# One order of the weight conversions for every block, single-block experts included

## The chip, the cores and the metric

The kernel runs on one core of a Trainium2 chip. The time is that of one execution on the device in microseconds (us). Three runs of the kernel before gave 2883.24, 2887.31 and 2889.01 us, median 2887.31 us. The profile is of one execution of its own, which took 2882.61 us.

## The reference, cut to what matters

The program is one layer of a diffusion backbone. A token mixer (gated DeltaNet and a gMLP) comes first and isn't touched by the change. The second sub-layer is a mixture of experts, and the change is in its loop. 1024 tokens of width 1024 each choose 4 of 32 experts, the assignments are sorted by expert and cut into blocks of one expert each, and every block is computed as

```python
gu = xblk @ w_gu[e] + b_gu[e]              # 1024 -> 2048
gate = jnp.minimum(gu[:, ::2], SWIGLU_LIMIT)
up = jnp.clip(gu[:, 1::2], -SWIGLU_LIMIT, SWIGLU_LIMIT)
act = (up + 1.0) * gate * jax.nn.sigmoid(SWIGLU_ALPHA * gate)
return act @ w_down[e] + b_down[e]         # 1024 -> 1024
```

The results are scaled by the gates and added up per token. All of it is float32.

## The kernel before, in words

**Blocks.** A block holds 64 rows of one expert. With these inputs there are 82 blocks for 32 experts. The experts are ordered so that busy and little used ones alternate: 7, 1, 7, 1, 6, 1, 5, 1, 4, 1, 3, 1, 3, 1, 3, 1, 3, 1 blocks, and then 3 and 2 in turn, and 2. So nine experts have a single block (blocks 7, 15, 22, 28, 33, 37, 41, 45 and 49, counted from 0), and each stands between two with more blocks. A block that is the first of its expert is called new here.

**Precision.** TensorE multiplies in float16 with each operand split into a high and a low half, and three products for each (high by high, high by low, low by high). So each weight chunk of 1 MB that arrives from memory in float32 is converted twice: ScalarE (ACT) writes its high half (line 1147 for gate-up, line 1153 for down), and after that VectorE (DVE) writes the low half as the difference (lines 1686 and 1691). An expert has 8 gate-up chunks, `k` from 0 to 7, and 4 down chunks. The halves of only one expert are held: the high half of chunk `k` may be overwritten when TensorE has done chunk `k` of the last block that used the old one.

**Loads.** SyncE (SP) issues the loads, strictly in order: gate-up chunks at line 587 into five staging buffers, down chunks at line 591 into four. A chunk's load goes out when the low half of the chunk that was last in its staging buffer is written. After an expert's chunks 5, 6 and 7 (which wait for its own low halves 0, 1 and 2) come chunks 3, 4, 0, 1, 2 of the next expert, in this order, each behind the low half 3, 4, 5, 6 or 7 of the expert before it.

**Turns.** Each engine runs the same loop over blocks, turn `t` from 1, with its own order of work.
- TensorE (PE): the 8 chunks of gate-up of block `t` (lines 2192 to 2194), the transposes of the gathered rows of block `t + 1` (line 2180), the transposes of the result of an earlier block (line 2219), then the 4 down chunks of block `t - 1` (lines 2209 to 2211). Gate-up of a block waits for the low half of each chunk, for its rows (`copy_xT`) and for VectorE's reading of the block before it.
- VectorE, with block `t + 1` as the one read: low halves of block `t + 2` if that one is new; the reading of gate-up (`read_gate_up`, line 1724); the clamps and the product of SwiGLU (lines 1730 to 1734); further low halves of `t + 2`; low halves of down of block `t + 1` if that one is new.
- ScalarE: the row index of a later gather; high halves of `t + 2`; `copy_xT` (line 1171), which can run once TensorE has transposed; more high halves; SiLU (line 1179), which waits for VectorE's first clamp; the remaining high halves; the high half of the activation (line 1184); the copies of results (lines 1189, 1196); high halves of down of `t + 1`, for a block with no new one behind it ahead of line 1184, otherwise at the end of the turn.
- GpSimd (POOL): the gather of rows (line 803), the low half of the activation (line 816), the scatter of results (line 810).

**The two orders.** `new1` says that block `t + 1` is new and `new2` that block `t + 2` is. The chunks of `t + 2` are converted in turn `t` only if `new2` is 1. With `new1` 0, ScalarE converts chunks 0 to 3 ahead of `copy_xT`, chunk 4 ahead of the SiLU, 5 to 7 behind it; VectorE converts 0 to 3 ahead of the reading and 4 to 7 behind SwiGLU. With both 1 (block `t + 1` is a single) ScalarE converts chunk 0 ahead of `copy_xT`, chunk 1 ahead of the SiLU and 2 to 7 behind it, and VectorE chunk 0 ahead of the reading and 1 to 7 behind SwiGLU. Each call of `next_gate_up` is a branch on its condition.

Of the kernel before, what the change touches and what calls it, by code (L numbers as in the profile page):

```python
# [41 lines left out]
GK, DK = 8, 4  # L42
# [71 lines left out]
def hybrid_block(nc, x, c, ctx_in, c_ctx, w_ada, b_ada, norm_g, w_in, conv_w, a_log, dt_bias,  # L114
# [3 lines left out]
    with es:  # L118
# [720 lines left out]
        def _(act):  # L839
# [293 lines left out]
            def flag(t):  # L1133
                return act.value_load(meta[0:1, bass.ds(t + NEW_AT, 1)], min_val=0, max_val=1)

            def rank_before(t):
                return act.value_load(rank_of[0:1, bass.ds(t - 1, 1)], min_val=0, max_val=NE - 1) + 1

            def flags_and_ranks(t):
                code = act.value_load(code_of[0:1, bass.ds(t, 1)], min_val=0, max_val=256 * NE - 1)  # L1140
                new1, new2, r1 = (code >> 1) & 1, (code >> 2) & 1, ((code >> 3) & (NE - 1)) + 1
                return new1, new2, r1, r1 + new1

            def high_gate_up(t, r, k):
                act.wait_ge(s_gst[k % GS], (r * 2 + (k // GS)) * 16 + 16 if k % GS + GS < GK else r * 16 + 16)
                reached(act, s_gu, t, GK, k + 1 - GK)
                act.activation(ghi[k], gstage[k % GS].rearrange("p (f b) -> p b f", b=2), ACT.Copy,  # L1147
                               scale=WSCALE).then_inc(s_ghi, 1)
# [7 lines left out]
            def next_gate_up(t, wanted, r, part):  # L1156
                with act.If(wanted):
                    for k in part:
                        high_gate_up(t, r, k)
                act.sem_inc(s_idle, 1)  # L1160

            def next_down(t, wanted, r):
                with act.If(wanted):
                    for j in range(DK):
                        high_down(t, r, j)
                act.sem_inc(s_idle, 1)

            def copy_xT(t):
                act.wait_ge(s_tx, t + 1)
                reached(act, s_gu, t, GK, 0)  # L1170
                act.activation(xT, ps[:, BX, :].bitcast(F16).rearrange("p (j k t) -> p j k t", j=2, k=KD),  # L1171
                               ACT.Copy).then_inc(s_xc, 1)

            def name_rows(t):
                act.activation(idx[:, 0:1], slots[:, bass.ds(t, 1)], ACT.Copy).then_inc(s_ix, 1)

            def sigmoid(t):
                act.wait_ge(s_gc, t + 1)
                act.activation(sig_n, gate_n, ACT.Silu, scale=ALPHA / WSCALE).then_inc(s_sig, 1)

            def high_act(t):
                act.wait_ge(s_a, t + 1)
                reached(act, s_dn, t, DK, DK)
                act.activation(ah, act_n, ACT.Copy).then_inc(s_ah, 1)  # L1184

            def copy_yT(t):
                act.wait_ge(s_dn, t * DK + 2 * DK)
                reached(act, s_ty, t, 1, EMPTY)
                act.activation(yT, ps[:, BT, :].rearrange("p (c t) -> p c t", c=8), ACT.Copy,  # L1189
                               scale=1.0 / (ALPHA * WSCALE * WSCALE)).then_inc(s_yT, 1)  # L1190

            def scale_y(t):
                act.wait_ge(s_ty, t + (EMPTY + 1))
                reached(act, s_ys, t, 16, 0)
                act.activation(idx[:, 1:2], slots[:, bass.ds(t, 1)], ACT.Copy)
                act.activation(ysb[0:B, :], ps[0:B, BY:BY + 2, :].rearrange("p b c -> p (b c)"), ACT.Copy,  # L1196
                               scale=gtab[:, bass.ds(t, 1)]).then_inc(s_yc, 1)
# [53 lines left out]
            new2, r2 = flag(2), rank_before(2)  # L1251
# [8 lines left out]
            with act.Fori(1, MAXB) as t:  # L1260
                with act.If(t <= nprev):
                    new1, new2, r1, r2 = flags_and_ranks(t)
                    act.wait_ge(s_xg, t * 16 + 48)
                    act.sem_inc(s_idle, 1)
                    name_rows(t + 3)
                    next_gate_up(t + 2, new2 > 0, r2, range(1))
                    next_gate_up(t + 2, new2 > new1, r2, range(1, 4))
                    copy_xT(t + 2)
                    next_gate_up(t + 2, new2 + new1 > 1, r2, range(1, 2))
                    next_gate_up(t + 2, new2 > new1, r2, range(4, 5))  # L1270
                    sigmoid(t + 1)
                    next_gate_up(t + 2, new2 + new1 > 1, r2, range(2, 5))
                    next_gate_up(t + 2, new2 > 0, r2, range(5, GK))
                    next_down(t + 1, new1 > new2, r1)
                    high_act(t + 1)
                    copy_yT(t)
                    scale_y(t - 1)
                    next_down(t + 1, new1 + new2 > 1, r1)
# [16 lines left out]
        def _(dve):  # L1295
# [110 lines left out]
            for m in range(NG - G_QKV):  # L1406
# [16 lines left out]
                if 0 <= j < NQK:  # L1423
                    ct, (t0, n) = j // 3, SPANS[j % 3]
                    dve.wait_ge(s_rt, ct + 1)
                    r, t = norm[ct % 2][:, NORM0[j % 3]:NORM0[j % 3] + n], qkvT[:, ct, t0:t0 + n]
# [257 lines left out]
            def low_gate_up(r, k):  # L1684
                dve.wait_ge(s_ghi, r * GK + (k + 1))
                dve.scalar_tensor_tensor(glo[k], gstage[k % GS].rearrange("p (f b) -> p b f", b=2), WSCALE, ghi[k],  # L1686
                                         ALU.mult, ALU.subtract).then_inc(s_glo, 1)
# [6 lines left out]
            def flag(t):  # L1694
                return dve.value_load(meta[0:1, bass.ds(t + NEW_AT, 1)], min_val=0, max_val=1)

            def next_gate_up(t, wanted, r, part, old=0):
                with dve.If(wanted):
                    for k in part:
                        low_gate_up(r, k)  # L1700
                if old:
                    with dve.Else():
                        dve.wait_ge(s_glo, t * GK + part[0])
                        dve.sem_inc(s_glo, old)
# [52 lines left out]
            new2, r2 = flag(2), rank_before(2)  # L1757
# [5 lines left out]
            with dve.Fori(1, MAXB) as t:  # L1763
                with dve.If(t <= nprev):
                    code = dve.value_load(code_of[0:1, bass.ds(t, 1)], min_val=0, max_val=256 * NE - 1)
                    new1, new2, r1 = (code >> 1) & 1, (code >> 2) & 1, ((code >> 3) & (NE - 1)) + 1
                    r2, e = r1 + new1, (code >> 8) & (NE - 1)
                    next_gate_up(t + 2, new2 > 0, r2, range(1), GK)
                    next_gate_up(t + 2, new2 > new1, r2, range(1, 4))
                    read_gate_up(t + 1, e)  # L1770
                    swiglu(t + 1)
                    next_gate_up(t + 2, new2 + new1 > 1, r2, range(1, 4))
                    next_gate_up(t + 2, new2 > 0, r2, range(4, GK))
                    next_down(t + 1, new1, r1)
                    dve.sem_inc(s_idle, 1)
# [487 lines left out]
```

## Time and profile before

| | |
|---|---|
| runs, median (lowest to highest) | 2887.31 us (2883.24 to 2889.01) |
| the profiled execution | 2882.61 us, span 2880.8 us |
| TensorE matmul, busy | 2584.2 us, 90% of the span |
| TensorE weight load, busy | 2238.8 us, 78% |
| VectorE, busy | 1755.5 us, 61% |
| ScalarE, busy | 1550.8 us, 54% |
| GpSimd, busy | 761.7 us, 26% |
| DMA | 536.74 MB, 186 GB/s over the span |

A busy share is the time in which an engine had an instruction at work, over the whole span. Matmuls are pipelined, so their mean duration is longer than the distance from one to the next. The chain of waits counts, for the instruction that ended last, what released each step; since it is the one that ended last, it says little about a loop in the middle of the program, and the views of single stretches say more.

### The profile page before, as it was taken

How to read it: one execution, taken by the hardware profiler on the slowest of the kernel's cores; microseconds unless marked ns; L12 is line 12 of the kernel's file. 1: busy time of each engine (PE TensorE's matmuls, PEld its weight loads, DVE VectorE, ACT ScalarE, POOL GpSimd, SP SyncE). 2: the span in 40 equal slices, each digit the busy share in tenths (PEclk: the TensorE clock that was granted, in tenths of full speed). 3: DMA queues.
4: the chain of work that ended last, by engine and by line, in shares of the span. 5: the costliest groups of instructions: out<-in, count | busy, mean ns of one | idle time of the engine just before them, and what ended most of it. 6: DMA issues, size and time to landing. Idle time of an engine off the chain costs nothing. (4 is left out here: it accounts for less than half of the span.)

```text
span 2880.8 us, 132861 instructions
## 1 busy us (share of the span) xinstructions
PE 2584.2 (90%) x55873; PEld 2238.8 (78%) x55873; DVE 1755.5 (61%) x1936; ACT 1550.8 (54%) x1833; POOL 761.7 (26%) x586
## 2 busy tenths in 40 slices
PE   8999997898898886699999999998889999999993
PEld 2444556788888754598998998988888999999993
DVE  2344894544545477517264638577787767878883
ACT  3522543433333543517264647577777767768773
POOL 1201003543544212112222222232222322233221
PEclk9999998999999997799999999999999999999997
DMA  9500001000000222818365659698899887979975
GB/s 366 192 30 32 1 1 37 19 26 15 18 25 15 84 96 104 341 24 285 119 209 192 227 173 342 219 329 319 316 351 308 307 291 272 326 276 350 348 276 194
DMA packets 124477, 536.74 MB, mean 186 GB/s; under 512 B 12541, under 2 KB 13553, under 8 KB 91617
## 3 DMA queue, kind: packets, MB, share of 16 engines
q1 hardware_dynamic: 107120, 481.80, 44.6%
q0 software_dynamic: 14464, 47.79, 7.3%
q10 hardware_dynamic: 2832, 6.37, 0.6%
q8 instruction: 36, 0.59, 0.1%
q14 instruction: 25, 0.20, 0.0%
HBM read 496.99 MB, written 38.92 MB: 186 GB/s over the span
## 5 line engine op out<-in xcount | busy, mean ns | idle before, releaser
L2192 PE MATMUL ps<-qkv,weights 128*128 128x64 f16 x10496 | 939.7, 193 | 71.7 <-DVE weights L1686 37.4
L2192 PEld LDWEIGHTS ps<-qkv,weights 128*128 128x128 f16 x10496 | 922.2, 98 | 87.6 <-DVE weights L1686 43.9
L2193 PE MATMUL ps<-qkv,weights 128*128 128x64 f16 x10496 | 939.1, 193 | 2.3 <-issue 2.3
L2194 PE MATMUL ps<-qkv,weights 128*128 128x64 f16 x10496 | 939.1, 193 | 0.0
L2193 PEld LDWEIGHTS ps<-qkv,weights 128*128 128x128 f16 x10496 | 922.9, 98 | 2.4 <-issue 2.4
L2194 PEld LDWEIGHTS ps<-qkv,weights 128*128 128x128 f16 x10496 | 922.9, 98 | 0.0
L1686 DVE SCALAR_TENSOR_TENSOR weights<-hT,weights 128x2048 f16<-128x2048 f32 x256 | 592.5, 2373 | 170.3 <-ACT weights L1147 145.2
L1147 ACT ACTIVATE weights<-hT 128x2048 f16<-128x2048 f32 x256 | 523.2, 2098 | 75.1 <-DMA hT<-in_w_gu_dram 66.2
L2209 PE MATMUL ps<-qkv,weights 128*128 128x64 f16 x5248 | 472.0, 193 | 20.8 <-DVE weights L1691 18.6
L2209 PEld LDWEIGHTS ps<-qkv,weights 128*128 128x128 f16 x5248 | 461.4, 98 | 27.4 <-DVE weights L1691 23.0
L2210 PE MATMUL ps<-qkv,weights 128*128 128x64 f16 x5248 | 471.7, 193 | 0.0
L2211 PE MATMUL ps<-qkv,weights 128*128 128x64 f16 x5248 | 471.7, 193 | 0.0
L2210 PEld LDWEIGHTS ps<-qkv,weights 128*128 128x128 f16 x5248 | 461.0, 98 | 0.8
L2211 PEld LDWEIGHTS ps<-qkv,weights 128*128 128x128 f16 x5248 | 461.0, 98 | 0.0
L816 POOL TENSOR_TENSOR qkv<-qkv 128x512 f16<-128x512 f32 x82 | 154.2, 1880 | 739.8 <-ACT qkv L1184 739.8
L1691 DVE SCALAR_TENSOR_TENSOR weights<-qkv,weights 128x2048 f16<-128x2048 f32 x128 | 300.7, 2394 | 57.5 <-ACT weights L1153 57.5
L1724 DVE TENSOR_TENSOR qkv<-ps,same 128x1024 f32<-128x1024 f32 x82 | 100.1, 1221 | 284.3 <-PE ps L2194 267.9
L1153 ACT ACTIVATE weights<-qkv 128x2048 f16<-128x2048 f32 x128 | 237.1, 1905 | 31.4 <-DMA qkv<-in_w_down_dram 25.3
L1959 PE MATMUL ps<-weights 128*128 128x128 f32 x1920 | 245.7, 289 | 7.0 <-ACT weights L1046 5.3
L1959 PEld LDWEIGHTS ps<-weights 128*128 128x128 f32 x1920 | 235.7, 200 | 14.0 <-ACT weights L1046 8.7
L1171 ACT ACTIVATE qkv<-ps 128x1024 f16<-128x1024 f16 x83 | 84.7, 1020 | 277.4 <-PE ps L2180 277.4
L803 POOL DMA_INDIRECT qkv<-h_scratch,idx x84 | 113.2, 1347 | 428.0 <-PE ps L2180 332.0
(395 smaller groups left out, 3979.8 us busy)
## 6 DMA issues: line engine op xcount, KB each, us to landing
hT<-in_w_gu_dram SPq DMA_DIRECT2D x256, 1024.0 KB, 6.9
qkv<-in_w_down_dram SPq DMA_DIRECT2D x128, 1024.0 KB, 5.7
weights<-in_w_ada_dram SPq DMA_DIRECT2D x12, 2048.0 KB, 16.4
qkv<-in_w_in_dram SPq DMA_DIRECT2D x4, 2048.0 KB, 7.7
hT<-decay_rows SPq DMA_DIRECT2D x20, 256.0 KB, 3.3
hT<-beta_rows SPq DMA_DIRECT2D x20, 256.0 KB, 3.9
qkv<-in_x_dram ACTq DMA_DIRECT2D x8, 512.0 KB, 6.6
weights<-in_w_in_dram SPq DMA_DIRECT2D x2, 2048.0 KB, 14.5
```

The source lines that it names most:

```text
L816: pool.tensor_tensor(al, act_n, ah, ALU.subtract).then_inc(s_al, 1)
L1147: act.activation(ghi[k], gstage[k % GS].rearrange("p (f b) -> p b f", b=2), ACT.Copy, scale=WSCALE).then_inc(s_ghi, 1)
L1153: act.activation(dhi[j], dstage[j].rearrange("p (j n) -> p j n", j=2), ACT.Copy, scale=WSCALE).then_inc(s_dhi, 1)
L1686: dve.scalar_tensor_tensor(glo[k], gstage[k % GS].rearrange("p (f b) -> p b f", b=2), WSCALE, ghi[k], ALU.mult, ALU.subtract).then_inc(s_g ...
L1691: dve.scalar_tensor_tensor(dlo[j], dstage[j].rearrange("p (j n) -> p j n", j=2), WSCALE, dhi[j], ALU.mult, ALU.subtract).then_inc(s_dlo, 1)
L1959: last = pe.matmul(out[:, h, :], lhsT(h), rhs(h), start=True, stop=True)
L2192: pe.matmul(dst, ghi[k][:, b, c], xT[:, 0, k, :], start=first, stop=False, skip_group_check=True)
L2193: pe.matmul(dst, ghi[k][:, b, c], xT[:, 1, k, :], start=False, stop=False, skip_group_check=True)
L2194: last = pe.matmul(dst, glo[k][:, b, c], xT[:, 0, k, :], start=False, stop=end, skip_group_check=True)
L2209: pe.matmul(dst, dhi[j][:, i, c], ah[:, f, :], start=first, stop=False, skip_group_check=True)
L2210: pe.matmul(dst, dhi[j][:, i, c], al[:, f, :], start=False, stop=False, skip_group_check=True)
L2211: last = pe.matmul(dst, dlo[j][:, i, c], ah[:, f, :], start=False, stop=end, skip_group_check=True)
```

## The change

In the loop over blocks the conditions that tell the two orders apart are gone, and the order for `new1` 0 serves every new block. The diff is whole; the lines are those of ScalarE's loop and of VectorE's.

```diff
@@ ScalarE @@
                     name_rows(t + 3)
-                    next_gate_up(t + 2, new2 > 0, r2, range(1))
-                    next_gate_up(t + 2, new2 > new1, r2, range(1, 4))
+                    next_gate_up(t + 2, new2 > 0, r2, range(4))
                     copy_xT(t + 2)
-                    next_gate_up(t + 2, new2 + new1 > 1, r2, range(1, 2))
-                    next_gate_up(t + 2, new2 > new1, r2, range(4, 5))
+                    next_gate_up(t + 2, new2 > 0, r2, range(4, 5))
                     sigmoid(t + 1)
-                    next_gate_up(t + 2, new2 + new1 > 1, r2, range(2, 5))
                     next_gate_up(t + 2, new2 > 0, r2, range(5, GK))
                     next_down(t + 1, new1 > new2, r1)
                     high_act(t + 1)
@@ VectorE @@
                     r2, e = r1 + new1, (code >> 8) & (NE - 1)
-                    next_gate_up(t + 2, new2 > 0, r2, range(1), GK)
-                    next_gate_up(t + 2, new2 > new1, r2, range(1, 4))
+                    next_gate_up(t + 2, new2 > 0, r2, range(4), GK)
                     read_gate_up(t + 1, e)
                     swiglu(t + 1)
-                    next_gate_up(t + 2, new2 + new1 > 1, r2, range(1, 4))
                     next_gate_up(t + 2, new2 > 0, r2, range(4, GK))
                     next_down(t + 1, new1, r1)
                     dve.sem_inc(s_idle, 1)
```

## Rows read from the trace of the kernel before

**Rows 1.** The page's costliest groups: line, engine, operation, count, busy us, mean ns, idle before.

```profile
L2192 PE MATMUL ps<-qkv,weights 128*128 128x64 f16 x10496 | 939.7, 193 | 71.7 <-DVE weights L1686 37.4
L1686 DVE SCALAR_TENSOR_TENSOR weights<-hT,weights 128x2048 f16<-128x2048 f32 x256 | 592.5, 2373 | 170.3 <-ACT weights L1147 145.2
```

**Rows 2.** Windows from block starts: stretch, length, busy by engine, clock, DMA.

```profile
1546.02:1564.77 18.75, 18.52 (x601) 18.32 (x602) 2.68 (x4) 3.96 (x8) 3.57 (x3) 1.00 0.16 28
1339.30:1386.73 47.43, 38.70 (x1200) 37.07 (x1201) 39.01 (x23) 33.39 (x29) 11.08 (x6) 1.00 0.97 359
1499.23:1525.44 26.21, 20.26 (x600) 18.73 (x601) 24.89 (x14) 20.40 (x16) 5.72 (x3) 1.00 0.94 354
1525.44:1546.02 20.58, 18.73 (x601) 18.26 (x602) 12.85 (x10) 11.97 (x13) 5.36 (x3) 1.00 1.02 373
2203.64:2250.44 46.80, 38.68 (x1200) 37.05 (x1201) 38.67 (x23) 33.47 (x29) 11.50 (x6) 1.00 1.01 370
2401.90:2422.15 20.25, 18.70 (x600) 18.37 (x601) 15.50 (x11) 14.48 (x13) 4.44 (x3) 1.00 0.90 338
```

**Rows 3.** Timeline of VectorE around block 15 (a single): start, us, line, count, idle.

```profile
1479.23 9.86 DVE L1686 SCALAR_TENSOR_TENSOR weights<-hT,weights 128x2048 f16<-128x2048 f32 x4 [0.86 <-DVE qkv L1734]
1491.96 2.29 DVE L1686 SCALAR_TENSOR_TENSOR weights<-hT,weights 128x2048 f16<-128x2048 f32 x1 [2.86 <-ACT weights L1147]
1494.17 1.22 DVE L1724 TENSOR_TENSOR qkv<-ps,same 128x1024 f32<-128x1024 f32 x1
1496.55 0.69 DVE L1734 SCALAR_TENSOR_TENSOR qkv<-qkv 128x512 f32<-128x512 f32 x1 [0.36 <-ACT qkv L1179]
1497.90 15.50 DVE L1686 SCALAR_TENSOR_TENSOR weights<-hT,weights 128x2048 f16<-128x2048 f32 x7 [0.67 <-DVE qkv L1734]
1514.69 8.90 DVE L1691 SCALAR_TENSOR_TENSOR weights<-qkv,weights 128x2048 f16<-128x2048 f32 x4 [1.28 <-ACT weights L1153]
```

**Rows 4.** Timeline of ScalarE in the same stretch and one block on.

```profile
1489.86 2.07 ACT L1147 ACTIVATE weights<-hT 128x2048 f16<-128x2048 f32 x1 [3.87 <-DMA hT<-in_w_gu_dram]
1492.53 1.02 ACT L1171 ACTIVATE qkv<-ps 128x1024 f16<-128x1024 f16 x1 [0.61 <-PE ps L2180]
1496.91 8.04 ACT L1147 ACTIVATE weights<-hT 128x2048 f16<-128x2048 f32 x4 [0.39 <-DMA hT<-in_w_gu_dram]
1508.69 2.08 ACT L1147 ACTIVATE weights<-hT 128x2048 f16<-128x2048 f32 x1 [1.20 <-DMA hT<-in_w_gu_dram]
...
1534.64 1.91 ACT L1153 ACTIVATE weights<-qkv 128x2048 f16<-128x2048 f32 x1 [0.65 <-DMA qkv<-in_w_down_dram]
```

**Rows 5.** Timeline of ScalarE around block 45: third chunk of block 46.

```profile
2117.78 7.99 ACT L1147 ACTIVATE weights<-hT 128x2048 f16<-128x2048 f32 x4 [2.41 <-DMA hT<-in_w_gu_dram]
```

**Rows 6.** Timeline of VectorE there: first down chunk of block 45.

```profile
2134.99 8.90 DVE L1691 SCALAR_TENSOR_TENSOR weights<-qkv,weights 128x2048 f16<-128x2048 f32 x4 [1.59 <-ACT weights L1153]
```

**Rows 7.** Timeline of VectorE around block 59, a two-block expert's last.

```profile
2399.30 1.21 DVE L1724 TENSOR_TENSOR qkv<-ps,same 128x1024 f32<-128x1024 f32 x1
2401.67 0.69 DVE L1734 SCALAR_TENSOR_TENSOR qkv<-qkv 128x512 f32<-128x512 f32 x1 [0.36 <-ACT qkv L1179]
2403.22 9.86 DVE L1686 SCALAR_TENSOR_TENSOR weights<-hT,weights 128x2048 f16<-128x2048 f32 x4 [0.86 <-DVE qkv L1734]
```

**Rows 8.** Timeline of GpSimd in the same stretch.

```profile
2409.74 1.19 POOL L816 TENSOR_TENSOR qkv<-qkv 128x512 f16<-128x512 f32 x1 [11.70 <-ACT qkv L1184]
```

**Rows 9.** Waits between 1480 and 1546 us: who for whom, us, times, longest.

```profile
PE ps L2219 <- ACT qkv L1196: 1.4, 1, 1.4
```

**Rows 10.** Timeline of SyncE: the load of block 16's third chunk.

```profile
1489.34 0.33 SPq L587 DMA_DIRECT2D hT<-in_w_gu_dram  x1
```

**Rows 11.** Line 587 between 1475 and 1525 us: from issue to landing.

```profile
DMA to landing us min/median/max: 4.9/6.3/8.4
```

**Rows 12.** Window of the first 5.66 us of gate-up of block 1.

```profile
1205.44:1211.10 5.66, 5.66 (x107) 5.66 (x108) 5.52 (x3) 5.66 (x5) 3.14 (x1) 0.50 0.25 94
```

**Rows 13.** Timeline of TensorE at the start of that window.

```profile
1205.44 0.21 PE L2192 MATMUL ps<-qkv,weights 128*128 128x64 f16 x1 [4.78 <-DVEq L1704]
```

## The prediction

> **What bounds the kernel now.** I read the page first, then windows cut at the block starts, then the timelines of VectorE and ScalarE in the stretches that came out long, and last the waits and single rows. The page shows VectorE and ScalarE far from full over the span, yet the largest idle time of gate-up's matmuls is put down to VectorE's low halves [rows 1]. The windows show where: a plain block takes 18.75 us, of which TensorE is busy 18.52, while VectorE has 2.68 us of work [rows 2]. TensorE bounds those, and nothing that ScalarE or VectorE gains there counts. What is long is the blocks in which an expert was converted. The nine singles matter most. Call the single B and the new block behind it C. C and C + 1 together take 47.43 us in the first case and 46.80 in the last [rows 2]; all nine sum to 423.6 us against 9 x 37.5 = 337.5, so 86 us are lost, 70.3 of them in C (7.8 each) and 15.9 in C + 1 (1.8 each). In the case of block 16 these are 26.21 and 20.58 us [rows 2]. In C, VectorE is busy 24.89 of 26.21 us: it writes seven low halves in 15.50 us, 2.2 each, where TensorE needs at most 1.5 for a chunk (a plain block has 12 equal ones, 8 of gate-up and 4 of down, in 18.52 us), and from 1497.90 us on it has no pause until the down chunks [rows 3]. So the place to ask is when VectorE gets to the first down chunk of B (line 1691, 1514.69 us), since the reading of C and then gate-up of C + 1 (1525.44 us, 10.75 later) follow it without a gap.
>
> **What the change does to a single.** Only turns with both flags set change their order, and there are nine. The chunks that move ahead of the reading aren't there yet when they are wanted. Chunk 2 of C goes into the buffer that B's chunk 7 frees. B's last four low halves run from 1479.23 to 1489.09 us [rows 3], the load goes out at 1489.34 [rows 10], and ScalarE begins chunk 2 at H = 1496.91, having waited for the DMA [rows 4]; for block 46 it is 2117.78, again behind the DMA [rows 5]. Before, VectorE used this time: it read B at 1494.17 [rows 3], with SiLU and product, and did chunk 1. After, reading and `copy_xT` stand behind chunk 3.
>
> Step 1, the start. Behind SwiGLU VectorE idles 0.86 us where it passes a branch that isn't taken [rows 7] and 0.67 where it doesn't [rows 3]. The removed branch lets B's low halves, the load behind them and H come 0.2 us earlier: H' = H - 0.2.
>
> Step 2, the chain. High half of chunk 2: 2.1 us; low halves of 2 and 3: 2.2 each; reading at H' + 6.5 (1503.2 us here, not 1494.2). Reading to first low half behind SwiGLU: 3.73 us (1494.17 to 1497.90) [rows 3]. Then three low halves at 2.2, and a last one that I take at 3.2: four took 9.86 us where GpSimd's line 816 fell beside them [rows 7, 8], one microsecond over 4 x 2.2. ScalarE keeps ahead: SiLU about 1.7 us behind the reading, then three high halves, ending by H' + 15, so that line 816 starts near H' + 15.7 and the last low half at H' + 16.8. In all H' + 20.0 = H + 19.8 for the first down chunk.
>
> Step 3, the shift. Before, it came at H + 17.8 for block 16 [rows 3, 4] and H + 17.2 for block 46 [rows 5, 6]; over the nine 16.3 to 18.7, mean 17.15. So VectorE is 2.7 us later a case (bounds: 1.7 if the last low half is not stretched, 3.5 at the nine's early end), and gate-up of C + 1 with it.
>
> Step 4, TensorE in C. It begins gate-up of C 1.9 us behind the reading (as from 1514.69 + 8.90 to 1525.44), at 1505.1 instead of 1499.2 us, finds four chunks ready and then waits for the rest. Costed at nothing: it would need gate-up of C to end over 3 us later before its down chunks passed VectorE's.
>
> Step 5, what the shift swallows. The 1.8 us lost in C + 1 hang on the last down chunk of C: ScalarE takes it at 1534.64 behind its DMA [rows 4], only then come the copies and the scaling at line 1196, for which TensorE waits [rows 9]. The loads run without a pause from the low half of chunk 4 on (DMA share 0.94 to 1.02) [rows 2]. That low half comes 2.4 us later (H' + 10.2, against 1504.5). The queue then was already behind by about 1.4 us (6.3 us from issue to landing, at best 4.9) [rows 11], so the tail of the queue moves by less; between 0.9 and 2.4 I take 1.5. TensorE arrives 2.7 later, its work is ready 1.5 later, and of the stall 1.8 - 1.2 = 0.6 us stays. A single costs 2.7 + 0.6 - 1.8 = +1.5 us; nine, +13.5 us. The ends: +0.9 each if the queue's tail hardly moves (+8), +2.7 if the whole stall stays (+24).
>
> **The other new blocks.** Their order is the same; the branches are fewer. Behind two-block experts VectorE is the last as well: 20.25 us against 18.75 [rows 2]. There are nine such blocks; in seven the wait is for the last low half alone, which comes 0.2 us earlier, in one it is so in part, in one the DMA bounds. In two of them line 816 starts only 0.1 us ahead of this low half (2409.74 against 2403.22 + 6.6 = 2409.8) [rows 7, 8], and 0.2 us turn the order about, which saves 1.0 us more. I count one of the two: 8 x 0.2 + 1.0 = -2.5 us (bounds -1.5 and -6). Branches in plain turns are hidden behind TensorE; uncovered they would be 0.2 us a turn.
>
> By the Trainium skill (SBUF - State Buffer, "SBUF: two separate sides") VectorE and GpSimd share a port pair as an exclusive lock, and whichever starts first holds it for its instruction. The 9.86 us of rows 7 agree; by that rule the stretched last low half of step 2 is certain, and without it the shift would be 1.7 and not 2.7.
>
> **Sum.** +13.5 - 2.5 = +11 us: the profiled execution goes from 2882.6 to 2893.6, and the median, which lay 4.7 above it, from 2887.3 to 2898.3 us. In TensorE's waits nothing else changes.
>
> **Rivals.**
> A, all but absorbed: the DMA queue's tail doesn't move, as chunk 6's load goes out almost 3 us earlier than before; then TensorE's arrival decides, +0.9 x 9 - 2.5 = +6 us, 2893. For it: the queue is full either way. Against: it runs dry once between chunk 3 and chunk 4.
> B, nothing absorbed: the down loads move by all 2.7 us, +24 - 2.5 = +22, 2909. For it: every request behind chunk 4 is later by 2.4 to 2.7. Against: the backlog.
> C, the clock: TensorE stands 6 to 8 us ahead of gate-up of C. After an idle 4.78 us [rows 13] gate-up of block 1 ran at a granted 0.50 for 5.66 us [rows 12], the lower level of 1.2 GHz; in all nine pairs it is 1.00 [rows 2]. At half clock 5.66 us of work lose 2.8. Step 4's slack takes that up; if it were all paid, +25 us on top, 2923. The Trainium skill (TensorE: Matmul & The Clock Gate, "The HAM clock gate") has idleness halve the array's clock and sustained work restore it; by it the fall is to be expected in all nine, and what it costs is the price just given.
> D, the other side, faster: chunk 2's load lands sooner. Its wait is the only reason to be late. With 4.9 us from issue to landing [rows 11] instead of the 7.6 from issue to use that it now has, H' is 2.7 us sooner: the first down chunk is where it was, the loads behind chunk 4 are 0.3 us ahead, and the time is 0.3 x 9 + 2.5 = 5 us under before, 9 with the other blocks' lower bound; about 2880. It decides from 2.7 us on. Against: nothing in the change takes traffic from that load.
> E, no effect (the flags are never both set): nine single experts rule it out but for a misreading, 2887.
>
> **How the numbers follow.** Forecast 0.45, A 0.20, B 0.20, C 0.05, D 0.08, E 0.02. No change means within 0.2%, 5.8 us, about what a measurement of this kernel can tell. Forecast, B, C and half of A lie above it, less a little for the spread of the forecast itself: slower 0.76. The other half of A, E and the rest: same 0.16. D: faster 0.08. The range goes from just above no effect (2888) to a little past B (2912).
>
> **What would show it.** Right: in the nine turns VectorE reads B about 9 us later than before and idles ahead of chunk 2; gate-up of C starts 6 us late with four chunks at 1.5 us or less; line 1691's first row 2.7 us later; C + 1 near 19.3 us instead of 20.5; granted clock under 1 at the start of C. Wrong: C's first down chunk at the old distance or earlier, C + 1 still at 20.5 us, or chunk 2 taken by ScalarE at another distance from line 587's issue than 7.6 us. A change in plain blocks or outside the loop would overturn the account.

## The result

Four runs of the changed kernel took 2912.17 to 2926.70 us, median 2923.1; four of the kernel before, on the same chip, had a median of 2886.6. The ratio is 1.0125, 95% interval 1.0108 to 1.0141: slower, by 36.5 us, where the prediction had 11, and above its range, which ended at 2912 us. The profiled execution is the one of 2926.70 us (span 2924.9), 44.1 us over the span before; the accounts below are of these two. It lies 3.6 us above the median of its kernel and the one before 4.0 below its own, so 7.6 of the 44.1 us are the spread between executions, and which stretch they lie in isn't shown. In the page the idle time ahead of gate-up's matmuls rose from 71.7 us [rows 1] to 97.8, and its largest releaser is now VectorE's reading of gate-up, which stands at line 1721:

```profile
L2187 PE MATMUL ps<-qkv,weights 128*128 128x64 f16 x10496 | 951.5, 194 | 97.8 <-DVE qkv L1721 62.3
L1683 DVE SCALAR_TENSOR_TENSOR weights<-hT,weights 128x2048 f16<-128x2048 f32 x256 | 593.9, 2370 | 209.5 <-ACT weights L1147 187.5
```

As before, B is the single, C the new block behind it, and D the next expert behind that of C. The windows of the kernel after, cut at block starts (columns as in rows 2: stretch, length, busy time of TensorE's matmuls, of its weight loads, of VectorE, ScalarE and GpSimd, then granted clock, DMA share, GB/s): block 15 (B), 16 (C), 17 (C + 1), a plain block, C and C + 1 together in the first and the last case, C + 1 of another case (block 39), and two stretches inside blocks 15 to 17.

```profile
1486.85:1512.07 25.22, 18.53 (x601) 18.33 (x602) 18.78 (x10) 16.36 (x13) 7.72 (x3) 0.92 0.97 322
1512.07:1535.03 22.96, 20.35 (x601) 19.79 (x602) 21.88 (x14) 17.16 (x15) 8.36 (x3) 0.94 0.92 324
1535.03:1557.76 22.73, 19.97 (x601) 19.42 (x602) 12.78 (x10) 11.95 (x13) 5.41 (x3) 0.92 0.97 337
1564.77:1583.50 18.73, 18.50 (x605) 18.30 (x602) 2.68 (x4) 3.95 (x7) 3.57 (x3) 1.00 0.16 28
...
1347.21:1393.10 45.89, 40.81 (x1200) 39.64 (x1201) 34.67 (x23) 29.09 (x27) 13.73 (x6) 0.93 0.92 337
2251.95:2297.59 45.64, 40.92 (x1200) 39.70 (x1201) 34.68 (x23) 29.06 (x27) 13.78 (x6) 0.92 0.91 330
...
2006.71:2028.29 21.58, 18.72 (x601) 18.25 (x601) 12.79 (x10) 11.91 (x13) 5.42 (x3) 1.00 0.94 341
...
1508.10:1514.90 6.80, 2.83 (x55) 2.87 (x55) 5.72 (x7) 5.41 (x5) 0.00 (x0) 0.50 0.97 342
1549.00:1552.40 3.40, 2.94 (x32) 2.65 (x33) 2.98 (x5) 1.99 (x4) 3.04 (x2) 0.50 1.06 349
```

The plain block is what it was (18.75 us in rows 2). Block 15, a plain 18.75 before, takes 25.22; C, 26.21 before, is down to 22.96; C + 1, 20.58 before, is up to 22.73. So C and C + 1 together look shorter than before (45.89 against 47.43 in the first case), and whoever compares only these two finds a gain: the wait has moved in front of C. VectorE, ScalarE, SyncE and the loads behind it, for the case of block 16 (start us, us busy, line, count, idle before):

```profile
1485.44 9.86 DVE L1683 SCALAR_TENSOR_TENSOR weights<-hT,weights 128x2048 f16<-128x2048 f32 x4 [0.68 <-DVE qkv L1731]
1498.50 2.29 DVE L1683 SCALAR_TENSOR_TENSOR weights<-hT,weights 128x2048 f16<-128x2048 f32 x1 [3.20 <-ACT weights L1147]
1501.00 2.29 DVE L1683 SCALAR_TENSOR_TENSOR weights<-hT,weights 128x2048 f16<-128x2048 f32 x1 [0.20 <-ACT weights L1147]
1506.29 4.49 DVE L1683 SCALAR_TENSOR_TENSOR weights<-hT,weights 128x2048 f16<-128x2048 f32 x2 [3.00 <-ACT weights L1147]
1510.70 1.22 DVE L1721 TENSOR_TENSOR qkv<-ps,same 128x1024 f32<-128x1024 f32 x1
...
1514.45 9.86 DVE L1683 SCALAR_TENSOR_TENSOR weights<-hT,weights 128x2048 f16<-128x2048 f32 x4 [0.68 <-DVE qkv L1731]
1524.24 8.88 DVE L1688 SCALAR_TENSOR_TENSOR weights<-qkv,weights 128x2048 f16<-128x2048 f32 x4
1533.04 1.22 DVE L1721 TENSOR_TENSOR qkv<-ps,same 128x1024 f32<-128x1024 f32 x1
```

```profile
1496.41 2.06 ACT L1147 ACTIVATE weights<-hT 128x2048 f16<-128x2048 f32 x1 [4.18 <-DMA hT<-in_w_gu_dram]
1498.86 2.11 ACT L1147 ACTIVATE weights<-hT 128x2048 f16<-128x2048 f32 x1 [0.39 <-DMA hT<-in_w_gu_dram]
1504.21 3.97 ACT L1147 ACTIVATE weights<-hT 128x2048 f16<-128x2048 f32 x2 [3.25 <-DMA hT<-in_w_gu_dram]
...
1521.01 7.29 ACT L1153 ACTIVATE weights<-qkv 128x2048 f16<-128x2048 f32 x4
...
1545.36 1.91 ACT L1153 ACTIVATE weights<-qkv 128x2048 f16<-128x2048 f32 x1 [0.57 <-DMA qkv<-in_w_down_dram]
```

```profile
1495.55 0.33 SPq L587 DMA_DIRECT2D hT<-in_w_gu_dram  x1
...
1528.13 5.60 SPq L591 DMA_DIRECT2D qkv<-in_w_down_dram  x4
```

Chunk 2 is asked for at 1495.55 us and taken by ScalarE at 1504.21, and the reading of B, which now stands behind it, comes only at 1510.70, 1.37 us before gate-up of C. From 1514.45 us to its reading of C at 1533.04 VectorE has no pause. What TensorE waits for in the two long blocks, from the waits view, first between 1512.1 and 1535.1 us and then over the whole case:

```profile
PE ps L2187 <- DVE qkv L1721: 6.7, 1, 6.7
PE ps L2187 <- DVE weights L1683: 1.1, 1, 1.1
...
PE ps L2214 <- ACT qkv L1196: 2.5, 1, 2.5
```

The means over the nine cases, in us from the start of gate-up of B, read from the timelines:

| | before | after | change | predicted |
|---|---|---|---|---|
| ScalarE takes chunk 2 (H) | 17.38 | 17.60 | +0.22 | -0.2 |
| VectorE reads B | 13.73 | 24.09 | +10.4 | about +9 |
| gate-up of C starts | 18.75 | 25.45 | +6.7 | about +6 |
| first down chunk of B on VectorE | 34.53 | 37.63 | +3.10 | +2.7 |
| gate-up of C + 1 starts | 45.31 | 48.40 | +3.09 | +2.7 |
| last down chunk of C on ScalarE | 54.44 | 58.46 | +4.02 | +1.5 |
| down chunks of C start on TensorE | 59.83 | 63.89 | +4.06 | |
| gate-up of C + 2 starts | 65.82 | 70.69 | +4.87 | +1.5 |

The column "predicted" for the reading and for gate-up of C has what the text gave for block 16's case. There ScalarE took chunk 2 at 16.43 us, 0.95 before the mean; by the same chain from the mean the reading would come about 10 us later. Nine times 4.87 is 43.9 us. The other new blocks give back 2.4 us, what lies ahead of the loop and block 0 took 3.3 us more in this execution, and what follows the last block's start 0.7 less; that makes the 44.1 us.

### The profile page after: what moved, and what is told of

It is laid out like the page before. It is cut to its first block and busy times, and to the rows that moved or that the text cites. A ratio compares the mean times of both kernels' runs of the same rounds, so it can differ in the third digit from the quotient of the medians.

```text
span 2924.9 us, 132092 instructions
## 1 busy us (share of the span) xinstructions
PE 2602.9 (89%) x55873; PEld 2264.3 (77%) x55873; DVE 1756.2 (60%) x1936; ACT 1547.1 (53%) x1833; POOL 786.5 (27%) x586
## 3 DMA queue, kind: packets, MB, share of 16 engines
q10 hardware_dynamic: 2832, 6.37, 0.6%
## 5 line engine op out<-in xcount | busy, mean ns | idle before, releaser
L2187 PE MATMUL ps<-qkv,weights 128*128 128x64 f16 x10496 | 951.5, 194 | 97.8 <-DVE qkv L1721 62.3
L2187 PEld LDWEIGHTS ps<-qkv,weights 128*128 128x128 f16 x10496 | 932.5, 99 | 108.8 <-issue 92.6
L2188 PE MATMUL ps<-qkv,weights 128*128 128x64 f16 x10496 | 951.4, 194 | 2.0 <-issue 2.0
L2189 PE MATMUL ps<-qkv,weights 128*128 128x64 f16 x10496 | 951.2, 194 | 0.0
L2188 PEld LDWEIGHTS ps<-qkv,weights 128*128 128x128 f16 x10496 | 932.4, 99 | 2.2 <-issue 2.2
L2189 PEld LDWEIGHTS ps<-qkv,weights 128*128 128x128 f16 x10496 | 932.6, 99 | 0.0
L2204 PE MATMUL ps<-qkv,weights 128*128 128x64 f16 x5248 | 478.5, 194 | 12.7 <-DVE weights L1688 11.3
L2204 PEld LDWEIGHTS ps<-qkv,weights 128*128 128x128 f16 x5248 | 465.8, 99 | 17.2 <-DVE weights L1688 13.4
L2205 PE MATMUL ps<-qkv,weights 128*128 128x64 f16 x5248 | 478.3, 194 | 0.0
L2206 PE MATMUL ps<-qkv,weights 128*128 128x64 f16 x5248 | 478.2, 194 | 0.0
L2205 PEld LDWEIGHTS ps<-qkv,weights 128*128 128x128 f16 x5248 | 465.3, 99 | 0.9
L2206 PEld LDWEIGHTS ps<-qkv,weights 128*128 128x128 f16 x5248 | 465.3, 99 | 0.0
L816 POOL TENSOR_TENSOR qkv<-qkv 128x512 f16<-128x512 f32 x82 | 163.3, 1992 | 782.1 <-ACT qkv L1184 782.1
L803 POOL DMA_INDIRECT qkv<-h_scratch,idx x84 | 124.2, 1478 | 411.0 <-PE ps L2175 324.1
```

What stands on the lines that cost most here:

```text
L816: pool.tensor_tensor(al, act_n, ah, ALU.subtract).then_inc(s_al, 1)
L2187: pe.matmul(dst, ghi[k][:, b, c], xT[:, 0, k, :], start=first, stop=False, skip_group_check=True)
L2188: pe.matmul(dst, ghi[k][:, b, c], xT[:, 1, k, :], start=False, stop=False, skip_group_check=True)
L2189: last = pe.matmul(dst, glo[k][:, b, c], xT[:, 0, k, :], start=False, stop=end, skip_group_check=True)
L2204: pe.matmul(dst, dhi[j][:, i, c], ah[:, f, :], start=first, stop=False, skip_group_check=True)
L2205: pe.matmul(dst, dhi[j][:, i, c], al[:, f, :], start=False, stop=False, skip_group_check=True)
```

## The experiments

All are measured against runs of the kernel before on the same chip. The diffs are cut to the lines that matter (`...` marks a cut). Line numbers in an experiment can differ by one to four from those above.

**e1, the next expert's loads out of the way.** The kernel after; for singles SyncE issues D's five loads behind the four down loads of C:

```diff
+                        with sp.If(table(meta, t + 1 + NEW_AT, 1) > 0):
+                            load_gate_up_ahead(t + 1)
...
-                        load_gate_up_ahead(t + 2)
+                        with sp.If(table(meta, t + 1 + NEW_AT, 1) < 1):
+                            load_gate_up_ahead(t + 2)
```

> The changed kernel with SyncE's loads in another order: behind a single expert, the five loads of the expert after next (chunks 3, 4, 0, 1, 2 of D) go out behind the four down loads of C, not ahead of them. Theory 1 (the loss in C + 1 is the queue: C's down loads are asked for late and stand behind D's): the last down chunk of C is taken by ScalarE some 4 us earlier, C + 1 falls from 22.3 to 18.8 us in all nine cases, nothing changes in C: 2923 - 9 x 3.5 = 2891 us. Rival (the loss in C + 1 comes from the order of work on ScalarE and VectorE, or from the array's clock after the long wait ahead of C): C + 1 stays at 22.3, 2923 us.

2906.54 us, ratio 1.0061 (1.0043 to 1.0080): half of the loss by the medians (a third by the profiled executions, both the slowest of their four: B to C + 2 takes 69.07 us, not 70.69). C + 1 falls from 22.29 to 19.85 us in the mean, and its clock is whole (the third window; the second shows the DMA engines busy for 0.39 of C, where it was 0.92):

```profile
1506.94:1529.90 22.96, 21.00 (x600) 20.44 (x601) 21.89 (x14) 17.23 (x15) 8.22 (x3) 0.91 0.39 111
1529.90:1550.13 20.23, 18.72 (x600) 18.25 (x601) 12.78 (x10) 11.91 (x13) 5.41 (x3) 1.00 1.02 390
```

Theory 1 had named 18.8 us for C + 1 and 2891 us in all, so it got the direction and a half of the size. Of the 2.4 us, 0.8 are given back in B and C; the likely reason, not tested, is that D's burst of loads meets the next case. The last down load of C still needs 10.1 us from its request to ScalarE, with nothing of D ahead of it.

**e2, the same in the kernel before** (12 runs).

> The kernel before with the same order of loads as in e1. Theory 1: the 1.8 us that C + 1 loses in each of nine cases go, 2886.6 - 16 = 2871 us, faster than both kernels. Rival: the down loads of C are bound by their own requests (behind B's low halves of down), C + 1 stays at 20.5 us and the time at 2886.

2886.34 us, ratio 0.9990 (0.9979 to 1.0001). C + 1 gets 0.9 us shorter (20.51 to 19.59) and B and C together as much longer, so nothing is won, as the rival had it. The last down load takes 9.85 us from request to ScalarE where it took 10.8. So no more than 0.9 us of it is a queue behind other loads. The rest stays for four 1 MB loads asked for 2.2 us apart with nothing ahead of them (D's five follow, 2.9 us behind the last). This is the number that my step 5 lacked.

**e3 and e4, how many chunks ahead.** The kernel before with two, and with three, chunks of C ahead of `copy_xT` and the reading in a single, the others behind SwiGLU. The diff is VectorE's of e3; e4 has 3 in place of 2, and ScalarE's lines are changed in the same way:

```diff
-                    next_gate_up(t + 2, new2 > 0, r2, range(1), GK)
-                    next_gate_up(t + 2, new2 > new1, r2, range(1, 4))
+                    next_gate_up(t + 2, new2 > 0, r2, range(2), GK)
+                    next_gate_up(t + 2, new2 > new1, r2, range(2, 4))
...
-                    next_gate_up(t + 2, new2 + new1 > 1, r2, range(1, 4))
+                    next_gate_up(t + 2, new2 + new1 > 1, r2, range(2, 4))
```

> Chunks 0 and 1 ahead of the copy and the reading behind a single, 2 to 7 behind SwiGLU; the other blocks as before. Theory 2 (the change costs because the reading stands behind chunk 2, whose load isn't there; chunk 1's is): the reading of B comes at 16.5 us after the start of B's gate-up (before 13.7, changed kernel 24.1), TensorE still starts gate-up of C at 18.8, VectorE's first down chunk comes at 34.5 to 35.5 (before 34.5, changed 37.6), and the time is 2886 to 2895 us. Rival (each chunk put ahead of the reading costs about its third of the 36 us): 2899.

> Chunks 0, 1 and 2 ahead, 3 to 7 behind SwiGLU, behind a single; the other blocks as before. Theory 2: the whole cost is there as soon as chunk 2 stands ahead. The reading comes at 22 us, gate-up of C at 23.5 (2 us sooner than in the changed kernel), but the first down chunk at 37.6 to 38.5 as in the changed kernel: 2923 to 2933 us. Rival (what costs is TensorE's wait ahead of gate-up of C, with its clock): 2 us less a case than the changed kernel, 2905 us.

e3 took 2895.89 us, ratio 1.0025 (1.0014 to 1.0036), e4 2930.21, ratio 1.0144 (1.0126 to 1.0162). With chunk 1 ahead block 15 stays plain, with chunk 2 ahead it is 4 us over (the window of block 15 in e3, then in e4):

```profile
1477.46:1496.21 18.75, 18.52 (x601) 18.32 (x601) 15.07 (x9) 10.96 (x11) 7.47 (x3) 1.00 0.95 321
```

```profile
1486.69:1509.52 22.83, 18.52 (x600) 18.32 (x601) 16.73 (x9) 12.73 (x11) 7.50 (x3) 0.98 0.96 334
```

The total of e3 lies between the two theories (2886 to 2895 and 2899 us) and doesn't decide; e4 does: it costs 41 us over the kernel before, e3 7 and the change 36. So most of the price is at chunk 2, the first chunk that is loaded late, and it isn't a third for each chunk that stands ahead.

**e5 and e6, no wait for chunk 2.** Chunk 2's load is left out and its halves are made from chunk 3's buffer, in the kernel after (e5) and in the kernel before (e6), so that this part of the weights isn't the reference's:

```diff
-            AHEAD = (3, 4, 0, 1, 2)
+            AHEAD = (3, 4, 0, 1)
...
-                dve.scalar_tensor_tensor(glo[k], gstage[k % GS].rearrange("p (f b) -> p b f", b=2), WSCALE, ghi[k],
+                dve.scalar_tensor_tensor(glo[k], gstage[3 if k == 2 else k % GS].rearrange("p (f b) -> p b f", b=2), WSCALE, ghi[k],
```

> The changed kernel with chunk 2 of gate-up never loaded (31 to 32 MB less): its halves are made from chunk 3's buffer, which is full some 10 us earlier, so a wait for chunk 2's load can't occur. The result is not the reference's in that chunk. Theory 2 (the change costs because the reading stands behind a load that isn't there): ScalarE takes chunk 2 at 14 us after the start of B's gate-up instead of 17.6, the reading is at 20.8, VectorE's first down chunk at 34.3 (changed 37.6, before 34.5), and the whole 1.2% goes: the same time as e6 within 0.3%, 2875 to 2895 us. Rival (the order itself costs, as TensorE waits for the reading and its clock falls): at least 20 us over e6.

> The kernel before with the same left out as in e5 (chunk 2 never loaded, made from chunk 3's buffer). VectorE was never waiting for chunk 2 there: first down chunk at 34.0 to 34.5 as before; the queue is shorter by one load, so C + 1 may lose less. 2870 to 2889 us. Rival: a gain as large as that of e5 over the changed kernel (30 us), which would say that the load of chunk 2 binds both orders.

e5 took 2873.39 us, ratio 0.9950 (0.9931 to 0.9969), e6 2871.93, ratio 0.9945 (0.9925 to 0.9966). The two orders are equal once chunk 2 is there. The kernel before gains 16 us by the load left out; only what e5 gains beyond that, some 35 us, speaks of the change. In e5 VectorE goes through chunks 1, 2 and 3 without a pause and reads B at 1499.56 us, 20.4 behind the start of B at 1479.17:

```profile
1492.94 6.70 DVE L1684 SCALAR_TENSOR_TENSOR weights<-hT,weights 128x2048 f16<-128x2048 f32 x3 [0.21 <-ACT weights L1148]
1499.56 1.22 DVE L1722 TENSOR_TENSOR qkv<-ps,same 128x1024 f32<-128x1024 f32 x1
...
1503.31 9.87 DVE L1684 SCALAR_TENSOR_TENSOR weights<-hT,weights 128x2048 f16<-128x2048 f32 x4 [0.68 <-DVE qkv L1732]
```

Gate-up of C still starts late (block 15 takes 21.76 us, in e6 18.75) and its clock still falls (0.93 over block 16), and yet gate-up of C + 2 starts 65.28 us behind B in the mean of e5 and 65.19 in e6. A late TensorE and a clock halved around the start of C cost nothing by themselves. The kernels before and after say the same: from VectorE's first down chunk of B to gate-up of C + 1 it is 10.74 to 10.81 us in all nine cases of both, with C at a clock of 1.00 before and of 0.88 to 0.94 after.

**e7, keeping TensorE at work.** The kernel after with small matmuls in TensorE's two gaps, guarded by flags that TensorE reads from SBUF, four reads in each turn. The second of the two guards:

```diff
+                        with pe.If(new_flag(t) + new_flag(t + 1) > 1):
+                            fill(160)
```

> The changed kernel with matmuls that nobody reads (identity by identity, 64 columns) where TensorE stands idle in the nine cases: 160 of them behind the down chunks of A, ahead of gate-up of C, and 80 behind gate-up of C + 1, ahead of the transposes. They keep the array at work. Theory 1 (the array's clock costs nothing in C, as TensorE there waits for VectorE's last low half anyway, and 0.8 us a case in C + 1): granted clock 1.00 in C and C + 1, gate-up of C + 1 starts at 48.4 us as in the changed kernel, C + 1 0.8 us shorter, 2923 - 7 = 2916 us, up to 2923 if the fillers or the flags that TensorE reads for them cost something. Rival C of the prediction (the clock's fall is what made 11 us into 36): 2923 - 25 = 2898 us.

4393.28 us, ratio 1.5208 (1.5179 to 1.5237), and no answer on the clock, since the guard costs more than all it guards. A plain block, in which no filler runs (its 600 matmuls are there, no more), takes 33.87 us, of which TensorE is idle 12.4, and the clock falls to 0.80 as well. The largest waits have no releaser in the profile ("issue"):

```profile
1268.61:1302.48 33.87, 21.48 (x600) 20.98 (x601) 2.68 (x4) 3.95 (x7) 3.57 (x3) 0.80 0.11 20
```

```profile
PE ps L2187 <- issue: 8.3, 1, 8.3
PE ps L2221 <- issue: 2.1, 1, 2.1
```

**e8, ScalarE's half of the change alone** (one run). VectorE keeps its old order.

> ScalarE's half of the change alone, VectorE in the order of before (chunk 0, reading, SwiGLU, the rest). The reading is early again (13.8 us), but the copy of C's rows and the SiLU stand behind chunks 2, 3 and 4 on ScalarE. Theory 2: gate-up of C starts at 22 to 23 us, the SiLU is done at 25, VectorE's seven low halves begin at 27 and the first down chunk comes at 42 to 43, five us later than in the changed kernel: about 2980 us. Rival (only VectorE's order costs): 2889.

2958.83 us, 71 us over the kernel before where the whole change costs 36. That is 21 less than theory 2 had (2980), though its first down chunk of B comes where that put it (42.8 us behind B). VectorE reads B early, but its product waits for a SiLU that stands behind chunks 2 to 4 on ScalarE, and seven low halves follow:

```profile
1498.81 1.22 DVE L1721 TENSOR_TENSOR qkv<-ps,same 128x1024 f32<-128x1024 f32 x1
...
1510.68 0.69 DVE L1731 SCALAR_TENSOR_TENSOR qkv<-qkv 128x512 f32<-128x512 f32 x1 [9.86 <-ACT qkv L1179]
1512.04 15.51 DVE L1683 SCALAR_TENSOR_TENSOR weights<-hT,weights 128x2048 f16<-128x2048 f32 x7 [0.66 <-DVE qkv L1731]
```

The two halves have to go together: VectorE's new order, which puts four low halves under the same wait, gives back 3.98 us a case (74.67 against 70.69 from B to C + 2, one execution each).

**e9 to e11, the filler again, without reading a flag.** The guard is now on the loop's own counter and picks five of the nine cases (C = 34, 38, 42, 46, 50); the other four serve for comparison. e9 fills the gap ahead of gate-up of C, e10 the one ahead of the down chunks of C, e11 both; the two lines with `fill` are those of e11.

```diff
+                        fill(4, t & 3, 34, 52)
                         turn_y(t)
                         down(t)
+                        fill(11, (t + 2) & 3, 32, 50)
```

> The kernel after, and in five of the nine cases (block C = 34, 38, 42, 46, 50) TensorE runs 220 small matmuls (about 6 us) at the end of B's turn, where it otherwise stands 5 to 7 us ahead of gate-up of C; the other four cases (C = 8, 16, 23, 29) have none and serve for comparison. The loop gets one to three branches more a turn, whose price no run shows, so the single cases are compared and not only the total. Theory 1 (the fall of the clock ahead of gate-up of C costs nothing, since VectorE's eighth low half ends last there): the granted clock stays at 1.00 through gate-up of C in the five cases, gate-up of C ends at the same place, and gate-up of C + 1 starts 48.4 us behind B in both groups, within 0.3. Theory 2 (rival C of the prediction, the clock is the price): in the five cases gate-up of C + 1 starts 2 to 3 us earlier, which is 10 to 15 us in all.

> The kernel after, and in the same five cases TensorE runs 80 small matmuls (about 2.2 us) in C + 1's turn, between gate-up of C + 1 and the wait for ScalarE's line 1196, where it otherwise stands 2.5 us and the clock falls in three of these five cases. Theory 1 (this second fall costs 0.6 to 1.6 us where it occurs, as the trace of after lets one read from the distance between the down chunks of C and the next block): the granted clock stays at 1.00 there, the distance is 5.98 us in all five, and the five cases are together 2.5 to 4 us shorter; in the four without filler three or four keep 6.6 to 7.6 us. Theory 2 (the distance is longer for another reason, the late requests for the down weights): the clock stays up and the distance is still 6.6 us or more in three of the five.

> Both fillers at once, in the same five cases. Theory 1: as the second filler alone, the five cases 2.5 to 4 us shorter than in the kernel after and the first filler adds nothing. Theory 2 (clock is the price of the change): the five cases together 13 us or more shorter, each of them close to the 65.8 us of before for B, C and C + 1 together plus the 4.1 us - 2.8 us left.

e9 took 2952.26 us, ratio 1.0164 (1.0146 to 1.0182), e10 2937.78, 1.0125 (1.0108 to 1.0142), e11 2960.88, 1.0207 (1.0190 to 1.0224). The totals say little, as the guards lengthen every turn (a plain block 19.08 us in e10 and 19.50 in e9); the cases say more. In e9 block 16, without filler, runs at 0.91, block 38, with it, at 1.00:

```profile
1516.07:1539.42 23.35, 20.98 (x600) 20.42 (x601) 21.92 (x14) 17.57 (x15) 8.27 (x3) 0.91 0.95 342
1992.26:2013.21 20.95, 18.87 (x601) 18.43 (x601) 20.55 (x12) 14.99 (x14) 8.41 (x3) 1.00 0.89 309
```

But from VectorE's first down chunk of B to gate-up of C + 1 it is 11.17 to 11.22 us in the four cases with the fall and 11.37 to 11.66 in the five at full clock, and gate-up of C + 1 starts 47.49 and 47.44 us behind B. The full clock bought nothing here, but e9 isn't a clean test: the fillers and their guard ran past the gap, and in the five cases gate-up of C began 3.1 to 5.6 us behind VectorE's reading of B, not 1.36. Block 38 looks 2.4 us shorter than block 16 because it starts later (26.26 us behind B, not 24.56) and VectorE was earlier in that case (35.58, not 36.74). The clean comparison is the one above, of before and after.

e10 doesn't isolate the second gap. The clock stayed at 1.00 in C + 1 in all nine cases, filled or not, and the distance from the first down chunk of C to the next block was 6.37 to 6.93 us in all of them. In block 16's case it holds a stall of 0.5 us that the kernel after doesn't have (the first of these lines; the second, 0.2 to 0.3 us, it has too):

```profile
PE ps L2204 <- issue: 0.5, 1, 0.5
PE ps L2204 <- POOL qkv L816: 0.3, 1, 0.3
```

In the kernel after that distance is 5.98 to 5.99 us in the three cases where the clock stays up and 6.6 to 7.6 in the six where it falls. The windows of that distance in two cases, block 42 without the fall and block 34 with it:

```profile
2111.65:2117.63 5.98, 5.76 (x192) 5.66 (x193) 1.91 (x4) 0.82 (x2) 2.68 (x2) 1.00 0.95 329
1931.75:1939.09 7.34, 7.09 (x192) 6.99 (x193) 1.92 (x4) 0.84 (x2) 2.68 (x2) 0.80 0.87 280
```

The work and TensorE's idle time (0.2 us) are the same, and 7.34 us at a clock of 0.80 are 5.9 us at full clock; over the nine cases distance times clock is 5.8 to 6.0. So the whole of the 0.8 us a case is the clock's, 7.3 us in all. e3 and e4 agree: 5.98 to 5.99 us where the clock stays up, 6.8 to 7.6 where it falls. In e11 the five cases with both fillers are together 4.1 us shorter from B to C + 2 than in the kernel after, and the four without any 4.3 us: the 13 us of theory 2 aren't there, and the fillers gained nothing.

## Why the prediction was right in direction and wrong in size

**Step 1, the start: wrong by 0.4 us.** The removed branch is there (0.68 us behind SwiGLU instead of the 0.86 that rows 7 had), but the load of chunk 2 took 8.7 us from issue to use in the case of block 16, not 7.6, which was one of the prediction's signs of being wrong. In the mean the load goes out 0.14 us earlier and takes 8.90 us to its use, not 8.54 (the 7.6 was below the mean already), so H came 0.2 us later instead of 0.2 earlier. Why the load took longer isn't shown.

**Step 2, the chain: right.** From H to the reading it is 6.49 us (1504.21 to 1510.70), predicted 6.5; from H to the first down chunk of B 20.02, predicted 20.0. The last low half is stretched: the four behind SwiGLU take 9.86 us. The 19.8 of the text was 20.0 less the 0.2 of step 1.

**Step 3, the shift: right within the 0.4 us of step 1.** +3.10 us, predicted +2.7, inside its bounds of 1.7 and 3.5.

**Step 4, TensorE in C: right, and with it rival C falls.** The clock is 0.50 around the start of C in all nine, for 3.4 to 10.2 us, after TensorE stood 4.8 to 7.8 us. Gate-up of C still waits 0.35 to 1.08 us for the eighth low half in seven of the nine; in the two with the longest fall it doesn't, and the slack is used up. The down chunks behind it wait for VectorE in all nine, and gate-up of C + 1 starts 1.97 us behind VectorE's reading of C. Rival C had named 2923 us, which is the measured median to the microsecond, by a mechanism that costs nothing here (10.74 to 10.81 us at either clock; e5 against e6). That the numbers meet is chance. The Trainium skill (TensorE: Matmul & The Clock Gate, "The HAM clock gate") has idleness halve the array's clock; the trace agrees in all nine, and the runs add that it had no price where VectorE's work ended last.

**Step 5, what the shift swallows: this one failed.** It said that the loads behind chunk 4 run against a backlog, so that the last down chunk of C comes only 1.5 us later and 1.2 of the shift is swallowed. It came 4.02 us later. The landing times of line 591 around the down loads of C in block 16's case, lowest, median, highest, in the kernel before and after. The view before knows the landings of the first two loads alone (8.0 and 10.0 us; after, the same two take 9.6 and 11.3), so the medians aren't to be compared:

```profile
DMA to landing us min/median/max: 8.0/9.0/10.0
```

```profile
DMA to landing us min/median/max: 9.6/11.4/11.9
```

The backlog was there, and it was used up before it mattered. D's chunk 4 is asked for behind low half 4 of C, 3.6 us later than before, in this case and in the mean; the prediction had 2.4, counted from block 16's case, whose H was early, and without step 1's 0.4 us; the queue, at work without a pause in the kernel before, runs partly dry ahead of that request (the 4 us around 1516.98 us, after), and the load lands in 4.8 us where it took 6.8 (1507.04 to 1513.85 us).

```profile
1514.85:1516.85 2.00, 2.00 (x72) 2.00 (x70) 2.00 (x2) 2.00 (x2) 0.00 (x0) 0.99 0.72 303
1516.85:1518.85 2.00, 2.00 (x75) 2.00 (x72) 2.00 (x1) 2.00 (x2) 0.00 (x0) 1.00 0.51 115
```

The down loads of C aren't in that queue yet. Each waits for a low half of B's down chunks (line 591's rule), so the request of the last one moved by the whole shift of VectorE, from 43.67 to 46.75 us in the mean, +3.1. The first moved further, from 37.53 to 41.60: SyncE comes to it only 3.6 us after the issue of D's last load, which hangs on the end of C's eighth low half, and that end moved by more than the down chunks behind it, since VectorE had 1.28 us of waiting between the two in block 16's case [rows 3] and has none now. The four so stand closer behind D's loads, and the last takes 11.7 us from request to use and not 10.8; e2 puts what could have been saved there at 0.9 us in all. I had charged these loads with the shift of chunk 4's request instead of their own.

So the stall in C + 1 grew where I had it shrink. It was 1.76 us; to it come 4.02 - 3.09 = 0.93 for the loads and 0.81 for the down chunks of C where the clock falls, in all 3.5 (C + 1 takes 22.29 us). I had 0.6. Of the 3.4 us that a case cost over the forecast (4.87 - 1.5), 0.4 are step 1's, 1.2 the shift that wasn't swallowed, 0.9 the slower service and 0.8 the clock in C + 1. Over nine cases that is 30 us, between the profiled executions the whole miss but for the 3.3 us ahead of the first case; between the medians the miss is 25 us. Rival B, with nothing absorbed, had the right mechanism for the requests and was short (+24 us for the nine, not 43.9) by the slower service, by the 0.4 us of step 1 and by the clock in C + 1, which no rival named.

**The other new blocks: right in the sum, the mechanism not shown.** Predicted -2.5 us; measured, the nine blocks were together 12.69 us over plain ones before and 10.29 after, -2.4. But it isn't 0.2 us in most of them and 1.0 in one: the single blocks moved by -1.2 to +0.2 us, four of them up. And e1, which leaves these blocks as the kernel after has them, has 12.79. So the agreement can be luck.

**The account as a whole** stands on two comparisons. e5 and e6 agree to 0.05%, so the slowdown is the wait for chunk 2, with the reading now behind it; e1 takes away a third to a half of it without touching VectorE's order, so that part reaches the end through the loads of C's down weights. Open are why the clock falls in C + 1 in six cases of nine and not in three (TensorE stood 2.0 to 2.6 us ahead in the six, and 1.1, 2.4 and 2.6 in the three), and why the service of the down loads got slower by 0.9 us and not by less.

## What to carry to other kernels

A change that moves work ahead of a wait must be costed at every request that hangs on the work behind it: follow the rule of each later load to the instruction that releases it, and charge each with the shift of its own releaser, the slack that stood ahead of that releaser included. A busy share near 1.0 over 20 us doesn't show a backlog; the time from request to use, against that of the same loads with nothing ahead of them, does. And a number that fits a rival is no evidence for it: the median fell on 2923 us by another mechanism than the one that had named it.

## What the runs showed of the hardware

- Four 1 MB down loads asked for 2.2 us apart take 9.9 to 10.1 us from the last request to its use with no other weight load ahead of them (e2, e1), where a gate-up load takes 4.9 to 8.4 to land [rows 11].
- Control flow on TensorE cost much here. One more guard whose branch isn't taken, ahead of the down chunks, makes a plain block 19.08 instead of 18.75 us (e10); one at the turn's end makes it 19.50 (e9); four reads of a flag and nested branches over 240 matmuls in all make it 33.9, at a mean clock of 0.80 (e7).
- VectorE's low half takes 3.25 us instead of 2.29 where it begins while line 816 runs on GpSimd, in all 37 such cases of the kernel before and in no other. Line 816 takes 1.15 us by itself and 1.2 to 3.2 where a low half is at work when it starts (54 cases). The Trainium skill (SBUF - State Buffer, "SBUF: two separate sides") has the one that starts first hold the shared port for its instruction; the trace agrees in both directions, and puts VectorE's loss at one microsecond.
- The same kernel before took 2886.6 to 2889.1 us (medians) on some chips and 2901.1 on another (median of seven runs beside e9 to e11), which is 0.4%.
